# A two-block transformer forward pass on one core: side jobs, split order, first adaLN slabs and S5 table layout moved

## The reference, cut to what matters

```python
for layer in range(DEPTH):
    mod = (c_act @ ada_w[layer] + ada_b[layer])[:, None, :]
    shift_m, scale_m, gate_m, shift_f, scale_f, gate_f = jnp.split(mod, 6, axis=-1)
    h = _rmsnorm(x, norm_g[layer, 0]) * (1.0 + scale_m) + shift_m
    ... # mix = conv/retention @ w_out (layer 0), S5 and GLU (layer 1)
    x = x + gate_m * mix
    h = _rmsnorm(x, norm_g[layer, 1]) * (1.0 + scale_f) + shift_f
    x = x + gate_f * (jnp.square(jax.nn.relu(h @ w_fc1[layer])) @ w_fc2[layer])
```

## Time and profile before

| | us |
|---|---|
| median of 3 runs | 1243.11 (1242.74 to 1246.62) |
| the profiled execution | 1247.09 |
| its span in the profile | 1245.2 |
| PE busy / DVE busy / ACT busy / POOL busy | 1190.6 / 853.1 / 531.7 / 416.1 |
| first feed-forward, jobs f1.0.0 to kl4 | 199.3 to 319.6 |
| its second half, blocks 0 to 7 | 319.6 to 443.8 |
| S5 loop | 461 to 532 |

### The profile page before, as it was taken

The page is one execution under the profiler, slowest core; times in us unless marked ns, Lnnn a source line. Parts: engine busy times, 40 slices in busy tenths (PEclk is TensorE's granted clock), DMA queues, the critical chain, the costliest instruction groups (busy, mean ns, idle before and its releaser), DMA issues.

```text
span 1245.2 us, 24492 instructions
## 1 busy us (share of the span) xinstructions
PE 1190.6 (96%) x10700; PEld 1120.4 (90%) x10700; DVE 853.1 (69%) x953; ACT 531.7 (43%) x675; POOL 416.1 (33%) x575
## 2 busy tenths in 40 slices
PE   5999999979978998899999999999999999999998
PEld 5887788879978978899999999799889999999998
DVE  5799896856747769864896543657886466665633
ACT  2121235434222344543655433547489535534431
POOL 7999699999786205500000000100000022000000
PEclk9799999989998999999999999999999999999999
DMA  9982787768975585274465445345323445455441
GB/s 341 395 314 102 253 292 267 274 244 297 345 278 215 209 316 181 85 265 164 161 246 201 158 184 203 135 155 184 119 86 135 172 167 203 154 185 203 170 169 68
DMA packets 119291, 258.20 MB, mean 207 GB/s; under 512 B 5120, under 2 KB 17040, under 8 KB 119056
## 3 DMA queue, kind: packets, MB, share of 16 engines
q1 hardware_dynamic: 90224, 196.18, 44.5%
q10 hardware_dynamic: 25504, 46.81, 10.4%
q0 software_dynamic: 3456, 13.63, 2.8%
HBM read 241.93 MB, written 14.68 MB: 206 GB/s over the span
## 4 chain that ended last, share of the span: by engine, by line
PE 74%; POOL 8%; issue 2%; DVE 2%; ACT 1%; DMA 1%; SPq 0%; DVEq 0%; POOLq 0%; ACTq 0%
PE bank L1979 74%; POOL tabw L739 3%; POOL tabw L736 2%; POOL prep L744 1%; POOL tabw L744 1%; DVE ada_acc L1372 1%; DMA tabw<-s_tables 1%; DVE ring_split L1424 0%; POOL tabw L756 0%; DMA prep<-in_s_bc 0%; PE bank L2551 0%; POOL tabw L775 0%; ACT h_in L872 0%; DVE big_split L1585 0%; ACT ada_acc L1055 0%
## 5 line engine op out<-in xcount | busy, mean ns | idle before, releaser
L1979 PE MATMUL bank<-squares_split,ring_split 128*128 128x256 f32 x1056 | 300.1, 284 | 0.0
L1979 PEld LDWEIGHTS bank<-squares_split,ring_split 128*128 128x128 f32 x1056 | 204.2, 193 | 0.0
L1372 DVE SCALAR_TENSOR_TENSOR ada_acc<-ada_slot,cact,ada_acc 128x512 f32<-128x512 f32 x150 | 132.1, 881 | 5.2
L1979 PE MATMUL bank<-ada_slot_split,ring_split 128*128 128x256 f32 x432 | 122.3, 283 | 0.0
L1424 DVE TENSOR_TENSOR ring_split<-ring,ada_slot_split 128x2048 fp32r<-128x2048 f32 (+1 forms) x31 | 70.6, 2282 | 53.9 <-ACT ada_slot_split L917 53.9
L1979 PE MATMUL bank<-big_split,ring_split 128*128 128x256 f32 x352 | 99.5, 283 | 0.0
L829 POOL TENSOR_TENSOR y_cat<-y_cat,tmp 128x512 f32<-128x512 f32 x8 | 10.7, 1339 | 235.8 <-DVE tmp L1883 235.8
L815 POOL TENSOR_TENSOR squares<-squares 128x512 f32<-128x512 f32 x4 | 5.6, 1389 | 240.8 <-ACT squares L1131 194.5
L1979 PE MATMUL bank<-big_split,ada_slot_split 128*128 128x256 f32 x296 | 84.9, 287 | 0.0
L1979 PEld LDWEIGHTS bank<-ada_slot_split,ring_split 128*128 128x128 f32 x432 | 82.9, 192 | 0.0
L1424 DVE TENSOR_TENSOR ring_split<-ring,tabw_split 128x2048 fp32r<-128x2048 f32 x22 | 50.4, 2291 | 41.3 <-ACT tabw_split L917 41.3
(11 more groups left out here) (442 smaller groups left out, 3867.7 us busy)
## 6 DMA issues: line engine op xcount, KB each, us to landing
ring<-in_w_fc SPq DMA_DIRECT2D x32, 2048.0 KB, 8.8
ada_slot<-in_ada_w ACTq DMA_DIRECT2D x20, 2048.0 KB, 12.9
ring<-in_w_in SPq DMA_DIRECT2D x18, 2048.0 KB, 8.0
ring<-in_w_ffn_gate SPq DMA_DIRECT2D x5, 2048.0 KB, 7.7
ring<-in_w_ffn_up SPq DMA_DIRECT2D x5, 2048.0 KB, 8.2
ring<-in_w_ffn_down SPq DMA_DIRECT2D x5, 2048.0 KB, 7.8
ring<-in_w_out SPq DMA_DIRECT2D x4, 2048.0 KB, 7.9
ring<-in_w_branch SPq DMA_DIRECT2D x3, 2048.0 KB, 8.7
```

The costliest lines, as they stand in the source:

```text
L1372: stt(acc, w[:, i, :], cact[:, i:i + 1], acc, ALU.mult, ALU.add)\
L1979: return pe.matmul(*args, skip_group_check=True, **kw)
```

## The change

- The two useless matmuls ahead of ada3 go. For chunk 3 PE takes slabs 0 and 1, from the first half of the load, and DVE slabs 2 to 7.
- kl0 stands after wo0.3, not before it. In the first feed-forward wt2, wt3, wt4 come after jobs 4, 9, 13 (were 3, 6, 10) and kl1, kl2, kl3 after jobs 2, 7, 11 (were 1, 5, 9). In the blocks, wt5, wt6, wt7 come after blocks 1, 3, 5 (were 0, 2, 4), kl5 and kl6 after blocks 2 and 4 (were 1, 3), and kl7 between the two halves of block 7 (was after block 5).
- DVE does ada_acc(10) in one piece right after split_low(2), ada11 comes one job earlier, and chunk 13 is loaded after job 4, not 5.
- In the loop over blocks ACT makes the activations' high part first, then unit, chunk load, unit, S5 copies; DVE makes `b_low` first, then one unit, the chunk's bias, half of ada_acc, the other unit, the other half.
- In the S5 loop ACT writes the decay rows two steps further ahead, one after the gelu and one after the copies of z.
- The tables of powers are laid out (c n t) in place of (n c t), so that a table goes from DRAM in one run of 4 KB for each partition.

```diff
 EARLY_ADA = 4
-KEEP_BUSY = {"ada3": 2, "f1.0.0": 2, "uu0": 4}
+KEEP_BUSY = {"f1.0.0": 2, "uu0": 4}
 DVE_SLABS = 6
+PE_SLABS = {k: (0, 1) if k == EARLY_ADA - 1 else (6, 7) for k in range(EARLY_ADA)}
...
-ADA_AFTER = {3: 10, 6: 11, 8: 12, 11: 13, 15: 14}
-ADA_LOAD_AFTER = {2: 12, 5: 13, 7: 14, 10: 15, 12: 16, 14: 17}
-ADA_HALVES = {0: (10, 0), 1: (10, 1), 2: (11, 0), 4: (11, 1), 5: (12, 0), 6: (12, 1), 7: (13, 0), 9: (13, 1),
+ADA_AFTER = {3: 10, 5: 11, 8: 12, 11: 13, 15: 14}
+ADA_LOAD_AFTER = {2: 12, 4: 13, 7: 14, 10: 15, 12: 16, 14: 17}
+ADA_HALVES = {1: (11, 0), 2: (11, 1), 4: (12, 0), 6: (12, 1), 7: (13, 0), 9: (13, 1),
               10: (14, 0), 11: (14, 1), 12: (15, 0), 13: (15, 1)}
-WT_AFTER = {3: 2, 6: 3, 10: 4}
-KL_AFTER = {1: 1, 5: 2, 9: 3, 15: 4}
+WT_AFTER = {4: 2, 9: 3, 13: 4}
+KL_AFTER = {2: 1, 7: 2, 11: 3, 15: 4}
 SIDE_ADA = {0: 15, 1: 16, 2: 17, 3: 18, 4: 19, 5: 20}
-SIDE_WT = {0: 5, 2: 6, 4: 7}
-SIDE_KL = {1: 5, 3: 6, 5: 7}
+SIDE_WT = {1: 5, 3: 6, 5: 7}
+SIDE_KL = {2: 5, 4: 6}
...
             "ro0", "ro1", "ada6", "rr0", "rr1", "mu", "g1", "var",
-            "wo0.0", "wo0.1", "ada7", "wt0.0", "wt0.1", "wo0.2", "ada8", "kl0", "wo0.3", "ada9", "ms1", "wt1.0", "wt1.1"]
+            "wo0.0", "wo0.1", "ada7", "wt0.0", "wt0.1", "wo0.2", "ada8", "wo0.3", "kl0", "ada9", "ms1", "wt1.0", "wt1.1"]
...
             jobs.append(f"kl{SIDE_KL[b]}")
-    jobs += [f"f2.0.{p}" for p in range(4)] + ["ada21", "ms2", "mms"]
+    jobs += ["f2.0.0", "f2.0.1", "kl7", "f2.0.2", "f2.0.3", "ada21", "ms2", "mms"]
...
         wout = [adas[1][:, 1280 * i:1280 * i + 1280].rearrange("p (n r m) -> p n r m", n=8, r=2) for i in range(3)]
-        tabs = [v.rearrange("p (n c t) -> p n c t", n=8, c=3) for v in (tabw[:, 0:1536], tabw[:, 1536:3072], dreg[:, 0:1536])]
+        whole_tabs = [tabw[:, 0:1536], tabw[:, 1536:3072], dreg[:, 0:1536]]
+        tabs = [v.rearrange("p (c n t) -> p n c t", n=8, c=3) for v in whole_tabs]
...
                     sp.wait_ge(s("s5r"), 2 * (k - 3) + 2)
-                sp.dma_start(tabs[k % 3][:, :, 0:2, :], tab_d[k].rearrange("p (n c t) -> p n c t", n=8, c=2)).then_inc(s(f"tab{k % 3}"), 16)
+                sp.dma_start(whole_tabs[k % 3][:, 0:1024], tab_d[k]).then_inc(s(f"tab{k % 3}"), 16)
...
                 buffer = tabw[:, 1024 * (k % 2):1024 * (k % 2) + 1024]
-                tb = buffer.rearrange("p (n c t) -> p n c t", n=8, c=2)
+                tb = buffer.rearrange("p (c n t) -> p n c t", n=8, c=2)
...
             split_high(1)
+            squares(1, False)
             s5_lags_out(0)
-            squares(1, False)
...
             for b in range(FC2, 8):
-                for u in range(2 * (b - FC2), 2 * (b - FC2) + 2):
-                    split_high(FC + u)
...
                 act.activation(fc2_high(b), big3[:, 4 * b:4 * b + 4, :], ACT.Copy).then_inc(s("b_high"), 1)
-                if b in (2, 3, 5):
-                    s5_weights_out({2: 5, 3: 6, 5: 7}[b])
-                if b in (2, 4, 6):
-                    s5_lags_out({2: 5, 4: 6, 6: 7}[b])
+                split_high(FC + 2 * (b - FC2))
...
                     ada_load(act, 16 + b)
+                split_high(FC + 2 * (b - FC2) + 1)
+                if b in (3, 5, 7):
+                    s5_weights_out({3: 5, 5: 6, 7: 7}[b])
+                if b in (4, 6):
+                    s5_lags_out({4: 5, 6: 6}[b])
+            s5_lags_out(7)
...
                 act.activation(d_w[:, :, q, :], ps(f"dd{q}")[:, :].rearrange("p (k m) -> p k m", k=8), ACT.Copy).then_inc(s("ddc"), 1)
+            for n in (3, 4):
+                decay_row(n)
             for k in range(8):
-                for n in (2 * k + 3, 2 * k + 4):
-                    if n < 16:
-                        decay_row(n)
...
                 act.activation(y_blocks[:, k].rearrange("p q t -> p (q t)"), bank[6 + k % 2][:, 0:T], ACT.Gelu_apprx_tanh).then_inc(s("gel"), 1)
+                if 2 * k + 5 < 16:
+                    decay_row(2 * k + 5)
...
                 act.activation(z_hi[:, k, :], ps(f"z{k}")[:, 0:T], ACT.Copy).then_inc(s("z_high"), 1)
+                if 2 * k + 6 < 16:
+                    decay_row(2 * k + 6)
...
                     dve.wait_ge(s("cact"), 1)
+                slabs = [slab for slab in range(KT) if slab not in PE_SLABS.get(k, ())]
                 for i in range(first, min(end, n)):
-                    if i == 4 and k < EARLY_ADA:
+                    slab = slabs[i]
+                    if slab == 4 and k < EARLY_ADA:
...
                     if i == 0:
-                        ts(acc, w[:, 0, :], cact[:, 0:1], None, ALU.mult).then_inc(s("ada_part"), 1)
+                        ts(acc, w[:, slab, :], cact[:, slab:slab + 1], None, ALU.mult).then_inc(s("ada_part"), 1)
...
                         dve.wait_ge(s("ada_part"), links + i)
-                        stt(acc, w[:, i, :], cact[:, i:i + 1], acc, ALU.mult, ALU.add)\
+                        stt(acc, w[:, slab, :], cact[:, slab:slab + 1], acc, ALU.mult, ALU.add)\
...
             split_low(2)
+            ada_acc(10)
...
             for b in range(FC2, 8):
-                if b >= 4:
-                    ada_mod(13 + b)
-                split_low(FC + 2 * (b - FC2))
-                if b == 3:
-                    ada_acc(18)
-                split_low(FC + 2 * (b - FC2) + 1)
...
                 tt(big_lo[:, tiles, :], big3[:, tiles, :], fc2_high(b).bitcast(F32), ALU.subtract).then_inc(s("b_low"), 1)
+                split_low(FC + 2 * (b - FC2))
                 if b == 2:
+                    split_low(FC + 1)
...
                     ada_acc(17)
-                    ada_mod(16)
-                elif 4 <= b < 6:
-                    ada_acc(15 + b)
-            ada_acc(21)
+                    continue
+                ada_mod(13 + b)
+                if b < 7:
+                    ada_acc(15 + b, 0, KT if b == 3 else 4)
+                split_low(FC + 2 * (b - FC2) + 1)
+                if 3 < b < 7:
+                    ada_acc(15 + b, 4)
...
-            def rows_split(names, u0, b0, blocks, x_high, ready):
+            def rows_split(names, u0, b0, blocks, x_high, ready, between_halves=None):
...
                                     end(last)
+                        if b == blocks - 1 and half == 0 and between_halves:
+                            between_halves()
...
                 begin(f"ada{k}")
-                if f"ada{k}" in KEEP_BUSY:
-                    keep_busy(f"ada{k}")
-                early_slabs = range(DVE_SLABS, KT) if k < EARLY_ADA else ()
+                early_slabs = PE_SLABS.get(k, ())
...
                     pe.wait_ge(s("cact"), 1)
-                    pe.wait_ge(*ada_in(k))
+                    if early_slabs[-1] < 4:
+                        pe.wait_ge(s(f"first_half{k}"), 16)
+                    else:
+                        pe.wait_ge(*ada_in(k))
...
                         mm(ps(f"ada{k}")[:, i:i + 1], ada_slot(k)[:, slab, P * i:P * i + P], cact[:, slab:slab + 1],
-                           start=(i == 0 and slab == DVE_SLABS), stop=False)
+                           start=(i == 0 and slab == early_slabs[0]), stop=False)
...
             ada(8)
+            project("wo0.3", w, 2, yt3, no_wait)
             s5_lags(0)
-            project("wo0.3", w, 2, yt3, no_wait)
...
             rows_open(sums, "f2.0.", FC2, big3, lambda k: pe.wait_ge(s("fsq_act"), k // 2 + 1))
-            rows_split(sums, FC, FC2, 8, lambda k: fc2_high(k // 4)[:, k % 4, :], lambda k: pe.wait_ge(s("b_low"), k // 4 - FC2 + 1))
+            rows_split(sums, FC, FC2, 8, lambda k: fc2_high(k // 4)[:, k % 4, :], lambda k: pe.wait_ge(s("b_low"), k // 4 - FC2 + 1),
+                       lambda: s5_lags(7))
```

## The result

The changed kernel takes 1225.63 us, the median of four runs, beside 1243.34 for the kernel before in the same comparison (1242.74 to 1246.62, four runs). One of the four took 1656.56 us at a mean granted clock of 0.655 and is left out of the ratio; the other three lie between 1223.24 and 1225.93. The ratio is 0.9846, 95% interval 0.982 to 0.9871: faster, clear of the interval though by less than 2%, by 17.7 us where 26.2 were forecast. The profiled execution took 1225.93 us, with a span of 1223.9.

What follows compares the result with a forecast made beforehand. PE is busy 1190.6 of 1245.2 us, so only its idle time and slow clock can yield: 1.4 + 3.1 + 6.9 + 11.8 + 6.5 (clock) + 0.5 - 4.0 = 26.2, 1243.1 to 1217 us; range 1209 to 1229.

Steps and rivals of the forecast that it cites:

- Chunk 3, kl0 and wt1: From the start to f1.0.0: both edits together leave 1.4 us (bounds 0 to 2.4), with wt1 waiting for POOL's x part.
- The first feed-forward: Jobs from f1.0.0 on: the 3.1 us wait for ada_acc(10) and the 6.9 us at wt3 go, with the clock after them.
- What is late next: POOL: At wt4 and kl4: POOL, stretched 0.47 us per us of DVE, makes PE wait 4 us (bounds 0 and 10).
- Blocks 0 to 7: Ahead of block 3: with b_low and a unit before chunk 18, the 11.8 us wait and 2.0 of clock go.
- S5 loop and tables: S5 loop: ready decay rows win 0.5 of 3.6 us; the new table layout gives 0.
- What the new profile was to show: Listed signs: big_split and ada_acc waits gone, clock 1.00 from 200 to 445, block 7 ending near 418, c part over 18 us.
- the second: Rival: POOL loses one us per us of DVE, PE waits 12.6 us in all: 1228, half of that 1222; chance 0.20.
- the fifth: Rival: no wait at POOL at all and the decays count: 1210; chance 0.13.
- the fourth: Rival: DVE is late at block 3 after all, 11.8 + 2.0 us come back: 1231; chance 0.10.
- the third: Rival, slower: POOL's table instructions cost more in the new layout, 1259 at 0.2 us each; chance 0.04.
- the sixth: Rival: nothing is gained, each wait moves to the next slot: 1243; chance 0.03.
- the first: Rival called likeliest: the terms as summed, 1217; chance 0.50.

Runs made afterwards that it cites:

- e6: The changed kernel, with DVE's sums of chunks 10 to 15 over four slabs instead of eight: 1219.29 us, ratio 0.9803.
- e1: The changed kernel with the chunk 3 edit taken back (two idle matmuls ahead of ada3, PE takes slabs 6 and 7): 1223.26 us, ratio 0.9829.
- e3: The changed kernel with kl4 after block 0 instead of last ahead of the blocks: 1226.2 us, ratio 0.9858.
- e5: The kernel before with all moved S5 slots, ACT's chunk loads ahead of its S5 copies; front, tables, decays, DVE order old: 1224.0 us, ratio 0.9836.
- e7: The changed kernel with the chunk 3 edit undone, wt4 behind f1.0.14, wt5 and kl5 one block earlier: 1225.4 us, ratio 0.9848.
- e8: The changed kernel, chunk 3 edit undone, wt4 behind f1.0.14, kl4, kl6, wt7, kl7 behind blocks 0, 5, 6, 7: 1223.18 us, ratio 0.9831.
- e10: The kernel before with only the moved slots ahead of the blocks (kl0, wt2 to wt4, kl1 to kl3): 1235.32 us, ratio 0.9942.
- e9: The kernel before with only the moved slots in the blocks (wt5-wt7, kl5-kl7), ACT's loads ahead of its S5 copies: 1233.49 us, ratio 0.992.
- e4: The kernel before with only DVE's and ACT's new order in the blocks, all slots old: 1239.88 us, ratio 0.9965.
- e12: The kernel before with only the new table layout and the new order of decay rows: 1243.91 us, ratio 1.0.
- e2: The changed kernel with ACT's two copies of v ahead of the load of chunk 7: 1224.65 us, ratio 0.9842.

## Why the prediction was right and where it was off

The kernel is faster, 1225.63 lies in the range, and the mechanisms named hold for most of the gain. The sum was 8.5 us too large (26.2 against 17.7). That the range still holds 1225.63 is in part luck: it reached that far for a POOL that loses one us for each us of DVE, which e6 rules out, and what filled it was something else. By its own steps:

**Chunk 3, kl0 and wt1 (forecast 1.4 us won, f1.0.0 at 197.9).** This is the step that failed. The order on DVE and PE came as written, and PE came to av0 earlier: on average at 37.6 in the four traces with the new front, at 38.8 in the ten with the old one. But f1.0.0 came 1.3 us later than before. I let POOL alone bound this stretch, through wt1, and didn't ask who frees the banks between 40 and 195 us: ACT's copies stood behind a load that waits for DVE, so g0 could not start before 132.2, and the slack turned into 2.96 us idle and 1.7 us of slow clock. Nor was wt1 the gate: in all 14 traces f1.0.0 starts 8.1 to 9.1 us behind the start of ms1, and PE waits there 0.9 to 1.9 us for DVE's `h_in_split`. 2.7 us of the sum are missing here. How much the chunk 3 edit costs is less sure: 2.4 us by e1 alone, 1.4 by the averages (f1.0.0 at 200.7 in after, e3 and e6, at 199.3 in e1, e5, e7, e8 and e10, with 198.2 to 201.1 among the latter). The wait at wt1 of 1 to 2 us did not come either, because PE was late (x part 1 was ready at 194.6, wt1 came at 195.6).

**The first feed-forward.** f1.0.0 to the end of kl4 took 109.4 us where it took 120.4. The sum had 3.1 + 6.9 and the clock after them, less POOL's lag. The waits went as said, but the reason for counting `ada_acc(10)` was wrong: with POOL as the next bound, those 3.1 us seem only to be handed to it (e5 keeps the wait and is as fast; `ada_acc(10)` was not tried alone).

**What is late next: POOL.** Right in kind and close in size: 3.1 us waited against 4.0 forecast, c part 4 at 309.2 against 307.0. At wt4 it was 0.23 us where I had 2.1, because PE came late from the front; e1, with f1.0.0 at 198.2, waits 2.05 there. Its slope was 0.37 us per us of DVE over the stretch, under the 0.47 that I took from two c parts. What I left out is that such a wait has its own slow clock: 0.4 in kl4 and 8.0 x (1 - 0.70) = 2.4 behind it. The lag cost 5.9 instead of 4.0. By e6 a kernel in which POOL is nowhere late takes 1219.3, so even then 2 us of the forecast are missing. The Trainium skill ("SBUF — State Buffer", section "SBUF: two separate sides") has the port pair that DVE and GpSimd share as an exclusive lock; the 0.37 to 0.47 us measured here for each us of DVE are less than half of what a POOL blocked through all of DVE's busy time would lose.

**Blocks 0 to 7.** 113.4 us where it was 124.2: 10.8 won of 13.8, the difference being mostly POOL's 0.34 us at wt7 and the 2.4 us of slow clock behind kl4, told above. The cause was half right. I named two reasons, `b_low` ahead of the chunk and the load no longer behind kl5; e5 and e9 show that the second alone suffices, e4 that the two changes of order (which bring the second with them) would have done it too, and e4 and e5 that the order without the slots loses most of it at wt7 and kl7.

**S5 loop and tables (0.5 and 0).** 1.0 in the ledger, inside its scatter; e12 gives nothing.

**From trace to median.** The forecast subtracted 26.2 from 1247.1 and from the median alike. But that execution was one of the slow ones of its kernel by chance: wt3's wait was 6.9 there and 5.35 and 5.33 in e9 and e4, which have the same slots there (in e12, with the same slots, 4.88 stood at wt4 instead), block 3's was 11.8 against 11.04 and 11.06 in e10 and e12. That is 2.3 us of the difference. In the traces the kernel gained 21.3, in the medians 17.7. The 8.5 us are 2.7 at the front, 3.0 in the blocks, 3.6 here, less 0.8 that other terms gave.

**What the new profile was to show.** Right: the waits for `big_split` and `ada_acc` gone, the waits for decays gone with PE's stalls still there (9.2 us), no wait of DVE for a chunk in the blocks. A c part longer than 18 us came too (c part 2, some 22 us), but told nothing, since before it had taken some 20. Not so: the clock is 0.70 in the 8 us behind kl4 and 0.99 on average ahead of it, and block 7 ends at 423.4, not 418. POOL's table phase did end after 144, at 145.4, and cost nothing, since x part 1 was in time; e12 ended it at 142.5, so it isn't the layout.

Of the rivals, the second and the fifth are out by e6's slope and by the waits that are there; the fourth did not happen, the third is refuted by e12 and the sixth by the result. The time lies between the first (1217) and the second (1228), by neither's sum.

## What to carry to other kernels

Before a wait is counted as won, ask for every queue in the way who is next to be late: here the kernel with DVE's 3.1 us wait removed (e1) waited 3.0 us for POOL further on, and the one that kept it (e5) not at all, and both take the same (1223.26 and 1224.0 us). Side jobs placed in another engine's order do two things at once, they wait for their producer and they block what stands behind their consumer's copy; a slot that is too early can hold up a load that has nothing to do with it, as kl5 did with chunk 18. And a change in parts should be priced in parts: the slots alone gave the time of the whole change (1224.0 against 1225.63), the block order alone 4 us, the tables and decays nothing.

## What the runs showed that was not expected

Executions of one kernel differ by 3 to 11 us, and where the traces run the same code they differ most in two places: the start of av0 (37.35 to 40.60 us with the same front, mostly absorbed again at g0) and the S5 loop (59.2 to 64.8 us with the same code), where PE's stalls without a semaphore add up to between 5.8 (e2) and 10.0 us (e8). And PE's clock: after 2.01 us of idle time ahead of g0 its 32 matmuls took 7.15 us, after 2.08 us they took 8.83; at wt4 an idle time of 2.05 us was followed by 3.22 us in e1 and by 2.08 us in e2 for the same pair; and at wt7 in e4 1.74 us was already followed by 3.10. So no single figure of idle time decides it.
